# Modulation by stationary columns, head norms by token, rotated keys in gaps

## The reference, cut to what matters

```
mod   = silu(c) @ w_ada + b_ada            # 6 x 1024; the first 2 x 1024 (shift, scale) are needed first
mod_c = silu(c_ctx) @ w_ada + b_ada        # for the 256 context tokens, shift and scale only
h  = rms_norm(x,   norm1_g) * (1 + sc1)  + sh1       # 512 x 1024
hc = rms_norm(ctx, norm1_g) * (1 + sc1c) + sh1c      # 256 x 1024
z  = h @ w_in ; zc = hc @ w_in             # q_c, kv_c, k_rope, gq, gk, gv, gr, glow, gates
q  = rms_norm(q_c, g) @ w_uq               # latent attention, 8 heads, with rope on 32 features
k, v = rms_norm(kv_c, g) @ w_ukv           # for 768 tokens; softmax(q k^T * MLA_SCALE) v
# gated linear attention, 4 heads x 2 directions, chunks of 64 tokens:
o = intra-chunk + state part ; y = rms_norm(o, gla_norm_g) * silu(gr) ; y @ w_br
```

## Time and profile before

| | before |
|---|---|
| median of 3 runs | 3144.44 us |
| the profiled execution, its own time | 3140.14 us |
| its span | 3138.1 us |
| TensorE busy (PE) | 3035.6 us |
| DVE busy | 1426.4 us |
| ScalarE busy (ACT) | 684.1 us |
| GpSimd busy (POOL) | 2064.9 us |
| mean granted TensorE clock | 0.988 |

### The profile page before, as it was taken

How to read it: one execution, slowest core, us unless ns; L and a number is a source line. 1 busy time by engine, 2 the same in 40 slices (tenths; PEclk the granted TensorE clock), 3 DMA queues, 4 the chain that set the end, 5 groups by cost and what they waited for, 6 DMA issues and landing times.

```text
span 3138.1 us, 38618 instructions
## 1 busy us (share of the span) xinstructions
PE 3035.6 (97%) x13632; PEld 2470.7 (79%) x13632; DVE 1426.4 (45%) x1857; ACT 684.1 (22%) x1191; POOL 2064.9 (66%) x2056
## 2 busy tenths in 40 slices
PE   5899999899999999999999999999999999999998
PEld 3777668778887788888888888888888887888886
DVE  7878742377456664222335322255422246442222
ACT  3244751111002532111122111100211115421110
POOL 4632227666666677777767777777777776777774
PEclk8999999999999999999999999999999999999999
DMA  6611112222222222222322222222222222322221
GB/s 257 234 56 34 41 61 95 87 88 99 96 95 93 94 101 98 97 94 100 107 81 94 98 97 94 100 94 95 100 94 99 96 94 94 103 99 94 100 95 67
DMA packets 86170, 307.24 MB, mean 98 GB/s; under 512 B 9569, under 2 KB 10081, under 8 KB 85793
## 3 DMA queue, kind: packets, MB, share of 16 engines
q1 hardware_dynamic: 82512, 297.73, 27.7%
q10 hardware_dynamic: 3536, 7.80, 0.7%
HBM read 303.39 MB, written 2.10 MB: 97 GB/s over the span
## 4 chain that ended last, share of the span: by engine, by line
PE 89%; DVE 7%; ACT 2%; SPq 1%; issue 1%; DMA 1%; ACTq 0%; DVEq 0%
PE acc L1601 85%; PE acc L732 1%; DVE rec_rec_x L2024 1%; PE side L759 1%; DVE ada_more L1170 1%; SPq L537 1%; DMA xc<-in_ctx 1%; PE side L742 0%; DVE state L1310 0%; PE side L1601 0%; PE stat L1664 0%; DVE n_scaled L1147 0%; PE acc L653 0%; DVE rec_rec_x L2022 0%; DVE att_stat L1372 0%
## 5 line engine op out<-in xcount | busy, mean ns | idle before, releaser
L1563 POOL TENSOR_TENSOR w_lo<-w_raw,w_hi 128x512 fp32r<-128x512 f32 x513 | 669.8, 1306 | 1005.1 <-PE acc L1601 974.9
L1601 PE MATMUL acc<-h_hi,w_hi 128*128 128x512 f32 x2224 | 875.6, 394 | 29.2 <-ACT gq L875 11.6
L1601 PE MATMUL acc<-h_hi,w_lo 128*128 128x512 f32 x2224 | 868.1, 390 | 0.0
L1601 PE MATMUL acc<-h_lo,w_hi 128*128 128x512 f32 x2224 | 868.1, 390 | 0.0
L1564 POOL TENSOR_TENSOR w_lo<-w_raw,w_hi 128x512 fp32r<-128x512 f32 x513 | 708.9, 1382 | 0.0
L1601 PEld LDWEIGHTS acc<-h_hi,w_hi 128*128 128x128 f32 x2224 | 418.8, 188 | 129.8 <-issue 15.0
L1601 PEld LDWEIGHTS acc<-h_hi,w_lo 128*128 128x128 f32 x2224 | 419.1, 188 | 85.2
L1601 PEld LDWEIGHTS acc<-h_lo,w_hi 128*128 128x128 f32 x2224 | 419.2, 188 | 85.0 <-issue 1.9
L1552 POOL TENSOR_SCALAR w_hi<-w_raw 128x512 fp32r<-128x512 f32 x513 | 404.0, 787 | 37.3 <-DMA w_raw<-in_weights 37.3
L1993 DVE TENSOR_TENSOR x<-acc,x 128x512 f32 (+1 forms) x160 | 110.7, 692 | 661.8 <-PE acc L1601 661.7
L1601 PE MATMUL acc<-mlp_hid_hi,w_hi 128*128 128x512 f32 x1024 | 398.3, 389 | 0.0
(11 more groups left out here) (350 smaller groups left out, 3535.4 us busy)
## 6 DMA issues: line engine op xcount, KB each, us to landing
w_raw<-in_weights SPq DMA_DIRECT2D x513, 512.0 KB, 3.2
ada<-in_ada SPq DMA_DIRECT2D x36, 512.0 KB, 5.6
ada_more<-in_ada SPq DMA_DIRECT2D x10, 512.0 KB, 18.3
x<-in_x ACTq DMA_DIRECT2D x16, 256.0 KB, 6.8
out<-x SPq DMA_DIRECT2D x8, 256.0 KB, 2.2
cvec<-in_cvec ACTq DMA_DIRECT2D x1, 1024.0 KB, 6.0
ada_n<-in_ada SPq DMA_DIRECT2D x2, 512.0 KB, 17.4
xc<-in_ctx SPq DMA_DIRECT2D x1, 1024.0 KB, 16.7
```

Of the source, the lines that this page charges most:

```text
L1563: pool.tensor_tensor(w_lo[:, slot, 0:half], w_raw[:, slot, 0:half], w_hi[:, slot, 0:half].bitcast(F32), ALU.subtract)
L1601: ins = pe.matmul(out, lhs, rhs, start=start, stop=stop, skip_group_check=group)
```

## The change

1. **Transfers.** x goes in two halves of 1 MB, the first at the head of SP's queue, the second on ScalarE's. Panel 0 goes ahead of the last three ada pieces, panel 1 behind them, then the context, then `cvec`, now one vector of 512 KB. A new constant `c_cols` [128, 8, 32] (128 KB) holds the two condition vectors as columns, the other 30 columns are zero. The first sixteen ada pieces are rearranged in memory: natural layout, piece 4p + g holds rows 256p to 256p + 255 of the columns 512g to 512g + 511. Pieces 16 to 19 wait for nothing of DVE any more.
2. **Modulation.** TensorE makes shift and scale for both vectors: `c_cols` is stationary (32 columns), each ada piece moves, four column groups of 32 write four ranges of partitions of one bank; eight blocks of four f32 matmuls of 512 columns. ScalarE copies the bank, TensorE transposes it in four parts, DVE adds the bias. 32 DVE products go.
3. **First norms.** DVE sums the squares of x, TensorE sums over the partitions once. Eight products with 1/rms are made in place before the modulation is there; then one operation per tile in place, ScalarE rounds with one Copy, DVE subtracts. The context's squares have their own places and are summed on TensorE behind the first two output tiles.
4. **First two output tiles** are made side by side, the second two k behind the first (`first_two`).
5. **Norms with tokens on the partitions.** The square tiles are stationary and ones move, so a token's sum is on its own partition; root and reciprocal work on 4 to 13 columns. The queries' 1/rms goes into the scores' scale per query token (`score_scale`); the weight q_norm is applied while splitting. For the keys and the heads ScalarE puts 1/rms on the diagonal of an identity matrix (`key_diagonal`, `head_diagonal`), and TensorE spreads it over the partitions with ones (`keys`, `spread`).
6. **Order.** The last head's sum stands behind the fourth query tile, its spread behind the eighth. DVE takes out the context part of the keys and copies the rotated keys and queries between waits.

```diff
@@ order of the gated attention
     for u in range(GLA_STEPS):
+        if u % 2 == 1 and u > 1:
+            order.append(("spread", u // 2 - 1, 1))
         order += [("turned", u, 2), ("intra", u, 1), ("added", u, 1)]
...
+        if u == GLA_STEPS - 1:
+            order.append(("keys", 0, 2))
         order.append(("output", u, 0))
@@ SP
-            for m in range(ADA_FIRST):
+            sp.dma_start(x[:, 0:KT // 2, :], io["x"][:, 0:KT // 2, :]).then_inc(x_in, 16)
+            for m in range(ADA_FIRST - 3):
                 load_ada(m)
+            load_panel(sp, 0, 0)
+            for m in range(ADA_FIRST - 3, ADA_FIRST):
+                load_ada(m)
+            load_panel(sp, 1, 1)
             sp.dma_start(xc[:, :, :], io["ctx"]).then_inc(ctx_in, 16)
+            sp.dma_start(cvec[:, :], io["cvec"]).then_inc(vec_in, 16)
@@ TensorE, start
+            def ada_block(j):
+                for group in range(ADA_GROUPS):
+                    slot = ADA_GROUPS * (j // 2) + group
+                    pe.wait_ge(ada_in[slot], 16)
+                    ins = pe.matmul(ada_rows[32 * group:32 * group + 32, :], c_cols[:, j, :], ada_slot[slot][:, T * (j % 2):T * (j % 2) + T],
+                                    start=(j == 0), stop=(j == KT - 1), tile_position=(0, 32 * group))
...
+            for j in range(KT):
+                ada_block(j)
+                if j == 1:
+                    pe.wait_ge(summed, KT)
+                    pe.matmul(stat[:, :], ones[:, :], square_sum[:, :], start=True, stop=True).then_inc(first_stat, 1)
...
+                ins = pe.transpose(side[:, 1, P * b:P * b + P], mod_rows[:, P * b:P * b + P], identity[:, :])
+            first_two()
+            for k in range(KT):
+                pe.wait_ge(squared, KT + k + 1)
+                pe.matmul(stat[:, 0:C], ones[:, :], ctx_squares[:, k, :], start=(k == 0), stop=(k == KT - 1)).then_inc(summed, 1)
@@ TensorE, token sums and spread
+                for b in range(n):
+                    for k in range(tiles):
+                        ins = pe.matmul(out[:, P * b:P * b + P], low_square[:, at(k, b):at(k, b) + P], ones[:, :],
+                                        start=(k == 0), stop=(k == tiles - 1))
...
+                if name == "spread":
+                    pe.wait_ge(head_diag, i + 1)
+                    out = begin_out()
+                    pe.matmul(out[:, :], ones[:, :], square[:, i % 2, :], start=True, stop=True).then_inc(out_made, 1)
@@ ScalarE
+            def head_diagonal(h):
+                act.wait_ge(head_inverse, h + 1)
+                for b in range(4):
+                    ins = act.activation(square[:, h % 2, P * b:P * b + P], identity[:, :], ACT.Copy, scale=head_rstd[:, 1, b:b + 1])
@@ DVE
             def head_output(h):
-                link(dve.reciprocal(root[:, :], root[:, :]))
...
+                take(dve.scalar_tensor_tensor(out=o_norm[:, :], in0=gr[:, h % 2, :], scalar=col("gla_norm"),
+                                              in1=bank(o), op0=ALU.mult, op1=ALU.mult), o)
+                own(dve.tensor_tensor(o_norm[:, :], side[:, h % 2, :], o_norm[:, :], ALU.mult), gla_y, h + 1)
...
+            for pair in range(HEADS // 2):
+                o = OUT_KH + 2 * pair + 1
+                wait_made(dve, o)
+                dve.tensor_copy(k_t[0:64, 2 * pair, T:TC], bank(o)[0:64, 0:C])
+                take(dve.tensor_copy(k_t[0:64, 2 * pair + 1, T:TC], bank(o)[64:P, 0:C]), o)
+                if pair < 3:
+                    ins = dve.tensor_copy(k_t[64:96, pair, :], k_rope)
```

More of the change, by code:

```diff
@@ L81 @@
 LEAD = 16
+ADA_GROUPS = 4
+SECOND_LAG = 2
 KB = TC // P
@@ L123 @@
 OUT_GLA, OUT_QH = gla_outputs()
-OUT_GLA["sum", GH - 1] = OUT_QH + HEADS
-OUT_KH = OUT_QH + HEADS + 1
+OUT_QN = OUT_QH + 5
+OUT_GLA["sum", GH - 1] = OUT_QH + 4
+OUT_GLA["spread", GH - 1] = OUT_QN + 4
+OUT_KH = OUT_QN + 5
 OUT_V = OUT_KH + HEADS
@@ L576, in first_block_pe @@
             hc_parts = [(hc_hi[:, k, :], hc_lo[:, k, :]) for k in range(KT)]
[L578 to L587, removed]
+            def ada_block(j):
[4 more added lines that the diff above has]
+                                    start=(j == 0), stop=(j == KT - 1), tile_position=(0, 32 * group))
+                if j == KT - 1:
+                    ins.then_inc(ada_sums, 1)
@@ L610, in first_block_pe, with token_sums @@
             pe.wait_ge(lr_sq, 1)
[L611 to L615, removed]
+            def token_sums(tiles, n, at):
                 out = begin_out()
[L617 to L620, removed]
+                for b in range(n):
+                    for k in range(tiles):
+                        ins = pe.matmul(out[:, P * b:P * b + P], low_square[:, at(k, b):at(k, b) + P], ones[:, :],
+                                        start=(k == 0), stop=(k == tiles - 1))
                 ins.then_inc(out_made, 1)
+            token_sums(QL, 4, lambda k, b: T * k + P * b)
+            token_sums(KVL, 4, lambda k, b: QL * T + TC * k + P * b)
+            token_sums(KVL, KB - 4, lambda k, b: QL * T + TC * k + T + P * b)
             def gla_part(name, i):
@@ L677, in gla_part @@
                     out = begin_out()
-                    pe.matmul(out[:, :], ones[:, :], square[:, i % 2, :], start=True, stop=True).then_inc(out_made, 1)
+                    for b in range(4):
+                        ins = pe.matmul(out[:, P * b:P * b + P], square[:, i % 2, P * b:P * b + P], ones[:, :], start=True, stop=True)
+                    ins.then_inc(out_made, 1)
+                if name == "spread":
+                    pe.wait_ge(head_diag, i + 1)
+                    out = begin_out()
+                    pe.matmul(out[:, :], ones[:, :], square[:, i % 2, :], start=True, stop=True).then_inc(out_made, 1)
+                if name == "keys":
+                    pe.wait_ge(key_diag, 1)
+                    for c0, c1 in ((0, T), (T, TC)):
+                        out = begin_out()
+                        pe.matmul(out[:, 0:c1 - c0], ones[:, :], key_spread[:, c0:c1], start=True, stop=True)\
+                          .then_inc(out_made, 1)
             def gla_output(u):
@@ L1328, in first_block_dve @@
                     decays(u + 1)
+                if d == 1 and h:
+                    head_output(h - 1)
                 masked_scores(u)
@@ L2448, in first_table, with ada_tile @@
     }
+def ada_tile(w, m):
+    if m < ADA_FIRST:
+        pair, group = m // ADA_GROUPS, m % ADA_GROUPS
+        part = w[2 * P * pair:2 * P * (pair + 1), T * group:T * (group + 1)]
+        return part.reshape(2, P, T).transpose(1, 0, 2).reshape(P, D)
+    return w[:, P * m:P * m + P].T
 def first_constants(g):
@@ L2473, in first_constants @@
         "reset": np.broadcast_to(np.isin(np.arange(TC + 1), [*range(0, T + 1, CHUNK), TC], invert=True).astype(np.float32), (P, TC + 1)),
-        "ada": np.asarray(g["w_ada"][0]).T.reshape(6 * KT, P, D),
+        "cvec": np.broadcast_to(g["c"][0][None], (P, D)),
+        "ada": np.stack([ada_tile(np.asarray(g["w_ada"][0]), m) for m in range(6 * KT)]),
+        "c_cols": np.stack([g["c"][0].reshape(KT, P).T, np.asarray(g["c_ctx"]).reshape(KT, P).T] + 30 * [np.zeros((P, KT), np.float32)], 2),
     }
```

338 lines of the change are left out of this document (200 added, 138 removed).

## The result

| | before | after |
|---|---|---|
| median, us | 3144.5 (3139.3 to 3145.7, 4 runs) | 3115.0 (3113.4 to 3119.2, 4 runs) |
| profiled execution, its own time / span | 3140.1 / 3138.1 | 3113.8 / 3111.8 |
| mean granted clock | 0.988 | 0.993 |

The ratio is 0.9911, with an interval of 0.9894 to 0.9929: 29.5 us less by the medians, 26.3 by the two profiled executions. Forecast were 3117 and 24.1 less.

The account below looks back on a forecast made before the run. TensorE was taken as the bound, busy 97% of the span, with time only where it idles or runs at lower clock. Terms -19.4 + 1.5 - 4.5 - 1.7 = -24.1 gave 3116.0 to 3120.3, taken as 3117; own range 3107 to 3125.

Parts of the forecast that it names:

- Transfers: Start of kernel: 1.4 MB less ahead of the modulation columns is 3.5 us, last ada piece at 32.9.
- Columns: Modulation on TensorE: 32 f32 matmuls in four column groups, 2.6 us behind the last ada piece, ending at 35.5.
- First product of h: First tile of h: copy, transposes, two small DVE operations, then scale-and-shift, rounding and subtraction; 40.9 against 45.75 us.
- Pace of h: First two output tiles: three DVE steps at 2.7, four at 1.6 us; last h at 55.4, two tiles at 58.1.
- Context: Context half of h: without its DVE products, ready by 78 or 80, under 83.3; the 11.6 us wait goes.
- Clock behind it: Stretch after the context tile starts: TensorE no longer rests before it, so 6.3 us at clock 0.53 give back 3.0.
- Token sums: Sums with tokens on the partitions: 24 matmuls of 128 columns replace three groups, +1.5 us.
- Gated attention: Gated attention loop: 4.7 us more work, 6.8 new waits, less 12.6 idle and 3.4 lower clock: -4.5 us.
- Before the attention: Stage before the attention: two TensorE waits for ScalarE, 0.9 and 1.0 us, go; -1.7 us.
- columns one at a time: Rival, 12%: modulation columns do not run four groups together and end at 47, not 35.5; total 3127.
- The loop gives nothing: Rival, 15%: in the gated attention TensorE waits as long as before, with 4.7 us more work; total 3126.
- The exposed round trip: Rival, 3%: gated attention's head sum to scaling, 6.6 us over four engines, exposed whole four times, 26.4; total 3150.

Follow-up runs that it names:

- Its own experiment: `lined_up` with all 32 column matmuls at tile position (0, 0), into four banks, with four ScalarE copies in place of one; measured 3114.2 us.
- lined_up: The changed kernel without the last of its four small tiles (6 floats, filler), putting og_hi at byte 133504; measured 3108.0 us, ratio 0.9883.

## Why the prediction was right

In the total it was right, and errors of opposite sign helped: it missed 6.9 us of loss and undervalued the gated attention by 6.1 us. Up to the scores the sum was 9 us short: they stood at 319.0 us, not near 328, 33.2 sooner and not 24.1. That the total came within 2.2 us of the sum is luck; that it lies in the range is not, as neither error alone leaves it. Point by point:

*Transfers.* Forecast: the last ada piece at 32.9. It landed at 32.55.

*Columns.* Four groups run together, the bound that the two-group row could not show; they end at 34.5, not 35.5. The sum's middle value of 2.6 us behind the last piece was 1.9. The Trainium skill, TensorEngine Tiling (Array Packing), section Theoretical Speedup, with its factor of up to four for 32 or fewer columns, had this: the trace agrees, by starts 20 ns apart.

*First product of h.* Forecast 40.9, measured 38.9: 1.0 from the columns, and 1.0 because copy, transposes and the two small operations took 1.9 us where 2.8 stood in the sum. The two small ones took 0.17 and 0.18 although GpSimd ran its subtraction from 35.12 to 36.39; I had costed them by the earlier trace rows beside GpSimd.

*Pace of h.* The sum had 14.5 us from the first product to the last low part and measured were 12.7, with the contention of the earlier trace rows in it again: 1.50 and 1.66 us for operations of 0.54 and 0.69. The two tiles ended at 56.0 (58.1), the six at 81.1 (83.3). The size was 2 us off, the mechanism as forecast. The one-input step did not stay short beside GpSimd: twice it took 1.50 us, twice 0.83, and each time it ended 0.27 to 0.29 us after the operation of GpSimd that it had met, as in this pair:

```profile
40.33 1.72 POOL L1687 TENSOR_TENSOR w_lo<-w_raw,w_hi 128x512 fp32r<-128x512 f32 x1
40.84 1.50 DVE L1262 TENSOR_SCALAR x<-x,gain,mod 128x512 f32<-128x512 f32 x1
```

So the saving that I kept as a bound did not come. The rule that I weighed, of the Trainium skill, SBUF — State Buffer, section SBUF: two separate sides, has two-port modes in the lock as well, and I had counted inputs only. No row names the mode, but the quiet step takes 0.40 us for 256 columns and 0.54 for 512, the subtraction with two inputs 0.42 and 0.69: per column the step is twice as fast. The trace agrees with the rule if the step runs in such a mode.

*Context.* The new low parts of hc end at 80.1, 1.4 us before TensorE's first product of hc at 81.5: the margin was thin, and nothing waited. Forecast was an end by 78 or 80.

*Clock behind it.* 3.0 us expected, 2.4 found: from the context tile to the token sums 59.6 us in place of 62.0, and the clock is 1.00 from 81.5 on, where it was 0.53.

*Token sums.* +1.5 forecast, +0.2 measured: 24 matmuls of 128 columns in 5.45 us, 0.23 each, where 0.28 came from four small ones with a gap in them.

*Gated attention.* -4.5 forecast, -10.6 measured; the old waits were gone as expected. Two terms were mis-sized. New waits: 6.8 in the sum, 3.7 idle in the window; the spread's bank cost 1.1 us twice, where the sum had 1 three times, and the step without a fill and ScalarE's wait, 2.3 and 1.5 in the sum, cost 0.6 and less. Clock: 3.4 in the sum; TensorE's busy time fell by 1.8 us though 4.7 us of work were added, so 6.5. A clock of 0.95 over 124.4 us is 6.2: I had taken half of what my own row shows. (At equal clock 4.7 us of the stage's length come with it, since waits hide a part.) And the profiled execution of before was a mild one, with 13.7 us of low clock where the other has 27.3 and a stage 3.0 us longer. That is most of the 4.3 us between its time and the median.

*Before the attention.* -1.7, as forecast, and the two waits of 0.9 and 1.0 us are gone from it.

*The step that failed:* "Behind 354 us the change touches only a scale operand, and those 2784 us are taken as they are." They are 6.9 us longer. The new tiles stand in the change, with their sizes, ahead of every new tile that the next 600 us bring to TensorE. I counted them as operands and not as neighbours.

Of the rivals, columns one at a time is out: the trace has four together. Its own experiment puts it at 6.9 us at the two tiles, where I had priced it at 10. The loop gives nothing is out: 6.0 us at equal clock. The exposed round trip did not come: its pieces are the 2.2 us at `added`.

## What to carry to other kernels

When a change adds small tiles, add up what they take after rounding, and see whether the large tiles behind them still start at a multiple of 128 bytes: here four small tiles that take 32 bytes more than was counted cost 6.6 to 7.1 us of TensorE, in stages that the change does not touch, and taking the 32 bytes out gives the fastest kernel of this study (3108.0). When two halves of a change gain less together than the whole, look for a cost that each pays alone, by comparing unchanged stages. And take a stage's price at the lower clock from the window's own clock times its length, then look at a second execution before summing against one.

## What was not expected of the hardware

- An fp32r matmul that streams 512 columns starts 226.7 ns after the last when its streamed tile begins at a multiple of 128 bytes, 228.9 on average at 64 off, 233.3 at 32 off. A stationary tile of hc that begins 32 or 64 off makes it 232.4 and 233.1.
- TensorE's 1.2 GHz windows are not fixed by the kernel. With 14 filler matmuls at 35 to 38.6 us the window at 39 to 49 us was gone, and one of 10.3 us stood at 247, after more than 230 us of full clock. `lined_up` had one of 6.8 us at 249 without them, and two executions of the kernel before differ by 13.6 us of low clock in that stage. What sets these windows is open.
- Five executions of four kernels with the changed loop at full clock take 113.6 us in the gated attention, within 0.1 us.
